# One ScalarE weight half moved ahead of two copies in both layers, another moved between the squares of the second mixer's norm

## The chip, the cores and the metric

The program runs on one core of a Trainium2 chip. The metric is device time in microseconds (us), smaller is better. Engines are called PE (TensorE matmul), DVE (VectorE), ACT (ScalarE), POOL (GpSimd) and SP (SyncE, which here only issues transfers). A wait in the queue of one engine holds everything that stands behind it in that queue, and nothing else.

## The reference, cut to what matters

Two blocks run one after the other on 256 tokens of width 1024. The first has two layers with three attention branches each, the second has two mixers; behind the first mixer stands a dense feed-forward net, behind the second a mixture of eight experts.

```python
for i in range(2):                                   # first block
    h = x @ w_in                                     # q, k, v and gates of three branches
    ya = moba_attention(...); yb = mla_attention(...); yc = diff_attention(...)
    merged = ga * (ya @ w_a) + gb * (yb @ w_b) + gc * (yc @ w_c)
    r = ALPHA * x + merged @ w_o
    x = layernorm(r + sigmoid(r @ w_pg) * (p_i @ w_p))
for i in range(2):                                   # second block
    h = rmsnorm(x, norm_mix[i])                      # squares, mean over 1024, x ** -0.5
    x = x + hybrid_mixer(h, w_in[i], ...)
    h = rmsnorm(x, norm_ffn[i])
    x = x + (swiglu(h, ...) if i == 0 else moe_swiglu(h, ...))
return rmsnorm(x, norm_final)
```

All of it is float32. The kernel multiplies float32 by splitting each operand into a high part (rounded by a copy to another format) and a low part (what the rounding left), and adding three products: high by high, high by low and low by high.

## The kernel before, in words

Everything is held feature by token: a tile has 128 features by 256 tokens, and x is eight such tiles. Weights come in units of 1 MB (1024 rows by 256 columns) through `ring`, which has three slots. SP issues one load per unit, in the order of use, each when the unit that is three places ahead in the ring has been read for good (`slot_freed`, which for a split unit is a count of its finished low parts). For each unit of 256 columns ACT makes the high part in two halves of 128 columns (`split`, one copy of 128x1024 each, signal `hi_done`). POOL makes the low parts of the layers and of the dense net (`low`, line 3092, signal `lo_done`), DVE those of the mixers. High and low parts have two places, so ACT may write the unit that is two ahead of the one that PE uses: `after("mc0")` is the copy of the unit two behind group `mc0`, which is `az0`. Its first half waits until PE has used the first half of `mc0`, its second until all of `mc0` is done, and both wait for the unit's load (`landed`).

The order on every engine is written out by hand. PE's order in a layer is the table `ORDER1`; the piece in question reads `("mc0"), ("B", 1), ("M", 0), ("V", 1), ("A", 2), ("mc1"), ("mc2"), ("B", 2)`. Here `B n` turns the probabilities of batch n (six or twelve transposes into PSUM), `M` is the second half of `mc0`, `V n` multiplies the turned probabilities `pT` with the values (into PSUM bank 7), and `A n` makes the scores. `scores(n)` writes bank 7 again with its last four matmuls, and so waits before them for `y_ready`: ACT's copy of the result of `V n-1` out of bank 7 (`take_y`). `pv(n)` waits for `pT_ready`: ACT's three copies of the turned probabilities (`take_turned`).

The second mixer's norm starts when the last dense unit is added up. DVE adds the sums to `xT` in four steps, ACT squares them (`square(j)`, 128x512), PE forms the mean with a matrix of 1/1024 in 16 records (`ms`), eight matmuls of zeros follow (`keep_busy(7, 8)`), ACT makes Ln and Exp (`inv_std`), DVE scales x to `h` tile by tile, ACT makes the high part of `h` in four pairs (`high_parts`), and PE's first group `gg` waits for each pair before it uses it (`split_project_first`). The half in question is the second half of the weights of `gv`, the group behind `gg`. The first half has been made at the end of the dense net's loop.

Of the kernel before, what the change touches and what calls it, by code (L numbers as in the profile page):

```python
# [62 lines left out]
LOG_EXP = "natural_log_exp_and_others"  # L63
# [196 lines left out]
def build_kernel(nc, a, out):  # L260

    ctx = ExitStack()
    with ctx:
# [9 lines left out]
        def signal(name, per=0):  # L273
            return Signal(sem(name), per)
# [220 lines left out]
        def views(b, n=2):  # L495
            return bank[b][:, :].rearrange("p (t s) -> p t s", t=n)
# [3 lines left out]
        FD = FF // S  # L500
# [23 lines left out]
        SPLITS_M = len(SPLIT2) + 3 * FD  # L524
# [53 lines left out]
        def _(sp):  # L578
# [107 lines left out]
        ff_full, ff_t, ff_g, ff_raw, ff_high, ff_h, ff_down = (signal(n) for n in (  # L686
            "ffn_full", "ffn_tanh", "ffn_gate_done", "ffn_hidden", "ffn_hidden_high", "ffn_h_ready", "ffn_down_done"))
# [980 lines left out]
        def _(act):  # L1668
# [3 lines left out]
            def copy(dst, src, scale=1.0):  # L1672
                return nc.scalar.activation(dst, src, ACT.Copy, scale=scale)  # L1673

            def split(slot, landed_at, q_slot, free, halves=(0, 1), width=P):


                act.wait_ge(landed[slot].h, landed_at)
                for t in halves:
                    if free:  # L1680
                        free(t)
                    copy(half_of(whi[:, q_slot, :], t, width), half_of(ring[:, slot, :], t, width)).then_inc(
                        hi_done.h, 1)
# [3 lines left out]
            def split1(layer, q, halves=(0, 1)):  # L1687

                n = split_unit(layer, q)

                def free(t):
                    if q >= 2:
                        turn, before = layer, SPLIT1[q - 2]
                    elif layer:
                        turn, before = layer - 1, SPLIT1[q - 2]
                    else:
                        return
                    if half_width(before) == S:
                        other = half_width((SPLIT1 + SPLIT1)[q]) != S
                        G1.wait_full(act, turn, before[:2] + str(int(before[2]) + (1 if other else t)))  # L1700
                    elif half_width((SPLIT1 + SPLIT1)[q]) == S:
                        G1.wait_full(act, turn, before)
                    elif t == 0 and before[1] != "v":
                        act.wait_ge(used.h, layer * len(SPLIT1) + q - 1)
                    else:
                        G1.wait_full(act, turn, before)
                split(n % RING, 16 * (n // RING + 1), q % 2, free, halves, half_width((SPLIT1 + SPLIT1)[q]))

            def drain(layer, name, dst, scale=1.0, rows=slice(0, P)):
                b = G1.wait_full(act, layer, name)  # L1710
                copy(dst, views(b)[rows], scale).then_inc(dr_a.h, 1)
# [4 lines left out]
            def inv_std(dst, src, e, log, at_log):  # L1716

                fn(dst, src, ACT.Ln, bias=eps[:, e:e + 1]).then_inc(log, 1)
                act.wait_ge(log, at_log)
                return fn(dst, dst, ACT.Exp, scale=-0.5)  # L1720
# [15 lines left out]
            def layer_body(layer):  # L1736
# [9 lines left out]
                def take_turned(n):  # L1746
                    act.wait_ge(p_turned.h, p_turned.at(layer, n + 1))
                    maps = 2 if BATCHES[n][0] == "diff" else 4
                    for i, b in enumerate((4, 5, 6)):
                        ins = copy(pT[:, 0:maps, i * P:(i + 1) * P],  # L1750
                                   bank[b][:, 0:maps * P].rearrange("p (m q) -> p m q", m=maps))
                    ins.then_inc(pT_ready.h, 1)

                def take_y(n):
                    kind, b = BATCHES[n]
                    act.wait_ge(pv_full.h, pv_full.at(layer, n + 1))
                    t0 = {"moba": 0, "mla": 4, "diff": 8}[kind] + 2 * b
                    copy(y[:, t0:t0 + 2, :], views(7)).then_inc(y_ready.h, 1)

                def after(name, halves=(0, 1)):  # L1760

                    split1(layer, SPLIT1.index(name) + 2, halves)
# [58 lines left out]
                drain(layer, "dv0", dv[:, :, 0:S])  # L1821
                after("dv1")
                drain(layer, "dv1", dv[:, :, S:512])
                take_turned(1)

                def latent(i):
                    b = G1.wait_full(act, layer, f"mc{i}")
                    copy(cq[:, 2 * i:2 * i + 2, :], views(b))
                    fn(gates[:, 2 * i:2 * i + 2, :], views(b), ACT.Square).then_inc(dr_a.h, 1)

                after("mc0")
                take_y(1)
                latent(0)
                exps(2)
                latent(1)
# [124 lines left out]
            def square(j):  # L1960

                return fn(sq[:, 2 * j:2 * j + 2, :], xT[:, 2 * j:2 * j + 2, :], ACT.Square)

            for layer in range(LAYERS):
                layer_body(layer)

            def split2(i, free, times=0, halves=(0, 1)):

                n = first_units + split_at2[i]
                split(n % RING, times + 16 * (n // RING + 1), i % 2, free, halves)  # L1970
# [38 lines left out]
            def high_parts(k):  # L2009

                for n in range(4):
                    act.wait_ge(h_part.h, h_part.at(k, n + 1))
                    copy(hh[:, 2 * n:2 * n + 2, :], h[:, 2 * n:2 * n + 2, :]).then_inc(hh_ready.h, 1)

            def mixer(m):
                def drained2_at(name):

                    return d2a.at(m, G2.nth(G2.index(name)))

                if m:  # L2020
                    for j in range(4):
                        act.wait_ge(x_up.h, j + 1)
                        square(j).then_inc(sq_ready.h, 1)
                    act.preload_act_table_set(LOG_EXP)
                b = G2.wait_full(act, m, "ms")
                inv_std(rs2[:, 0, :], views(b)[:, 0, :], 0, d2a.h, drained2_at("ms")).then_inc(std_ready.h, 1)
                if m:
                    split2(SPLITS_M + 1, lambda t: act.wait_ge(ff_down.h, 4 * FD), halves=(1,))
                high_parts(2 * m)
                high2(m, "xb0")  # L2030
                b = G2.wait_full(act, m, "gg")
# [84 lines left out]
            def norm(n):  # L2116
# [12 lines left out]
                if n == 1:  # L2129
                    high_ffn(0, (1,))  # L2130

            mixer(0)
            norm(1)
            high_parts(1)
# [36 lines left out]
            with act.Fori(0, FF_LOOP) as jj:  # L2171
# [6 lines left out]
                for k in range(3, 5):  # L2178
                    high_loop(jj, k)
                high_loop(jj, 5, (0,))  # L2180
            mixer(1)

            def token_squares(half, t, to):
# [1006 lines left out]
```

## Time and profile before

| what | us |
|---|---|
| median of three runs | 2121.65 |
| lowest and highest of the three | 2121.0 to 2123.34 |
| the profiled execution: its own time | 2121.3 |
| the profiled execution: span from first to last instruction | 2119.5 |
| PE busy in that span | 2096.3 (99%) |
| DVE, ACT, POOL busy | 1416.4, 1295.4, 651.4 |

The profile is one execution with the start, length and releaser of every instruction. Times in its rows are microseconds from the start of the span. A row of the order of time merges like instructions: start, length, engine, source line, operation, output<-input, count, and in brackets the idle time ahead of it with what ended it. Since line 720 is a helper that issues nearly every matmul, and line 1673 one that issues every ACT copy, rows are told apart by the names of what they write and read.

### The profile page before, as it was taken

How to read it: one execution, taken by the hardware profiler on the slowest of the kernel's cores; microseconds unless marked ns; L12 is line 12 of the kernel's file. 1: busy time of each engine (PE TensorE's matmuls, PEld its weight loads, DVE VectorE, ACT ScalarE, POOL GpSimd, SP SyncE). 2: the span in 40 equal slices, each digit the busy share in tenths (PEclk: the TensorE clock that was granted, in tenths of full speed). 3: DMA queues.
4: the chain of work that ended last, by engine and by line, in shares of the span. 5: the costliest groups of instructions: out<-in, count | busy, mean ns of one | idle time of the engine just before them, and what ended most of it. 6: DMA issues, size and time to landing. Idle time of an engine off the chain costs nothing.

```text
span 2119.5 us, 33547 instructions
## 1 busy us (share of the span) xinstructions
PE 2096.3 (99%) x13311; PEld 1867.1 (88%) x13315; DVE 1416.4 (67%) x1437; ACT 1295.4 (61%) x1424; POOL 651.4 (31%) x316
## 2 busy tenths in 40 slices
PE   9999999999999999999999999999999999999998
PEld 8979999988999999999998888888888888888887
DVE  1555223346422774223777999999999999999997
ACT  4556545455544534444545777777777777777776
POOL 5717886726787204988101000000000000000000
PEclk9999999999999999999999999999999999999999
DMA  7434564625455425655447999999999999999995
GB/s 245 138 105 153 179 198 156 183 75 163 160 188 177 129 91 175 189 193 178 141 140 252 387 376 336 370 360 376 352 351 370 351 375 351 359 356 375 367 365 200
DMA packets 307633, 529.06 MB, mean 250 GB/s; under 512 B 11842, under 2 KB 152802, under 8 KB 307520
## 3 DMA queue, kind: packets, MB, share of 16 engines
q1 hardware_dynamic: 306496, 525.92, 70.9%
q8 instruction: 84, 1.38, 0.3%
q0 software_dynamic: 736, 1.00, 0.2%
q10 hardware_dynamic: 288, 0.52, 0.1%
q14 instruction: 29, 0.24, 0.0%
HBM read 525.84 MB, written 1.05 MB: 249 GB/s over the span
## 4 chain that ended last, share of the span: by engine, by line
PE 90%; POOL 3%; DVE 3%; ACT 2%; DMA 1%; issue 1%; SPq 0%; DVEq 0%; POOLq 0%
PE bank L720 88%; POOL weights_low L3092 3%; PE bank L1525 1%; DVE qb L2354 1%; DMA ring<-in_w_in_dram 1%; ACT sc L1670 1%; ACT weights_high L1673 0%; DVE sc L2362 0%; DMA ring<-in_w_ple_dram 0%; DVE h L2362 0%; PE bank L929 0%; PE bank L731 0%; DVE nmax L2389 0%; ACT expert_weights_high L1673 0%; ACT xT L1670 0%
## 5 line engine op out<-in xcount | busy, mean ns | idle before, releaser
L2354 DVE TENSOR_TENSOR expert_weights_low<-ring_experts,expert_weights_high 128x2048 fp32r<-128x2048 f32 x336 | 764.7, 2288 | 72.6 <-ACT expert_weights_high L1673 72.5
L1673 ACT ACTIVATE expert_weights_high<-ring_experts 128x2048 fp32r<-128x2048 f32 x336 | 646.4, 1924 | 166.3 <-PE bank L720 162.2
L3092 POOL TENSOR_TENSOR weights_low<-ring,weights_high 128x1024 fp32r<-128x1024 f32 x252 | 617.5, 2474 | 332.0 <-ACT weights_high L1673 218.8
L1673 ACT ACTIVATE weights_high<-ring 128x1024 fp32r<-128x1024 f32 x294 | 303.9, 1056 | 331.7 <-PE bank L720 293.0
L720 PE MATMUL bank<-x_high,weights_high 128*128 128x256 f32 x1024 | 229.8, 281 | 0.5 <-POOL weights_low L3092 0.4
L720 PE MATMUL bank<-x_high,weights_low 128*128 128x256 f32 x1024 | 226.2, 277 | 0.0
L720 PEld LDWEIGHTS bank<-x_high,weights_high 128*128 128x128 f32 x1024 | 183.6, 188 | 2.5 <-POOL weights_low L3092 0.8
L720 PEld LDWEIGHTS bank<-x_high,weights_low 128*128 128x128 f32 x1024 | 183.3, 188 | 0.5 <-issue 0.5
L720 PE MATMUL bank<-expert_weights_high,gathered_high 128*128 128x512 f32 x456 | 180.7, 396 | 0.4 <-DVE gathered_low L2362 0.4
L720 PE MATMUL bank<-expert_weights_high,gathered_low 128*128 128x512 f32 x456 | 177.8, 390 | 0.0
L720 PE MATMUL bank<-expert_weights_high,gathered_high_b 128*128 128x512 f32 x448 | 177.6, 396 | 0.0
L720 PE MATMUL bank<-expert_weights_high,gathered_low_b 128*128 128x512 f32 x448 | 174.7, 390 | 0.0
L720 PE MATMUL bank<-expert_weights_high,hidden_turned_low 128*128 128x512 f32 x440 | 171.3, 389 | 0.0
L720 PE MATMUL bank<-expert_weights_high,hidden_turned_high 128*128 128x512 f32 x440 | 171.2, 389 | 0.0
L720 PE MATMUL bank<-h_high,weights_high 128*128 128x256 f32 x704 | 164.0, 283 | 5.1 <-ACT h_high L1673 5.1
L720 PE MATMUL bank<-h_high,weights_low 128*128 128x256 f32 x704 | 161.6, 281 | 0.0
L720 PEld LDWEIGHTS bank<-h_high,weights_high 128*128 128x128 f32 x704 | 131.1, 192 | 7.7 <-ACT weights_high L1673 2.9
L720 PE MATMUL bank<-x_low,weights_high 128*128 128x256 f32 x1024 | 137.4, 277 | 0.0
L720 PEld LDWEIGHTS bank<-h_high,weights_low 128*128 128x128 f32 x704 | 130.6, 192 | 0.0
L720 PEld LDWEIGHTS bank<-x_low,weights_high 128*128 128x128 f32 x1024 | 126.3, 188 | 0.0
L720 PE MATMUL bank<-expert_weights_low,gathered_high 128*128 128x512 f32 x456 | 122.3, 390 | 0.0
L720 PE MATMUL bank<-expert_weights_low,gathered_high_b 128*128 128x512 f32 x448 | 120.0, 390 | 0.0
(338 smaller groups left out, 3724.7 us busy)
## 6 DMA issues: line engine op xcount, KB each, us to landing
ring_experts<-in_moe_w_gate_dram SPq DMA_DIRECT2D x112, 1024.0 KB, 6.0
ring_experts<-in_moe_w_up_dram SPq DMA_DIRECT2D x112, 1024.0 KB, 5.8
ring_experts<-in_moe_w_down_dram SPq DMA_DIRECT2D x112, 1024.0 KB, 5.4
ring<-in_w_in_dram SPq DMA_DIRECT2D x62, 1024.0 KB, 5.3
ring<-in_w_merge_dram SPq DMA_DIRECT2D x24, 1024.0 KB, 5.1
ring<-in_w_out_dram SPq DMA_DIRECT2D x14, 1024.0 KB, 5.1
ring<-in_ffn_w_gate_dram SPq DMA_DIRECT2D x11, 1024.0 KB, 5.4
ring<-in_ffn_w_up_dram SPq DMA_DIRECT2D x11, 1024.0 KB, 5.3
```

What stands on the lines that cost most here:

```text
L720: ins = pe.matmul(dst, w, x, start=start, stop=stop, skip_group_check=share)
L1525: ins = pe.transpose(bank[2][:, c * P:(c + 1) * P], hd[:, c * P:(c + 1) * P], ident)
L1670: return nc.scalar.activation(dst, src, func, **kw)
L1673: return nc.scalar.activation(dst, src, ACT.Copy, scale=scale)
L2354: return nc.vector.tensor_tensor(dst, x, z, op)
L3092: nc.gpsimd.tensor_tensor(half_of(wlo[:, q_slot, :], t, width), half_of(ring[:, slot, :], t, width), half_of(whi[:, q_slot, :], t, width). ...
```

## The change

Two places on ACT change. In both layers the first half of the copy for `az0` moves ahead of the three copies of turned probabilities, and the copy of y moves ahead of the second half. In the second mixer the load of the table for Ln and Exp moves ahead of the squares, and the second half of the weights of `gv` moves from behind the Exp to between the second and the third square.

```diff
                 drain(layer, "dv1", dv[:, :, S:512])
+                after("mc0", (0,))
                 take_turned(1)
+                take_y(1)
+                after("mc0", (1,))
 ...
-                after("mc0")
-                take_y(1)
                 latent(0)
                 exps(2)
...
                 if m:
+                    act.preload_act_table_set(LOG_EXP)
                     for j in range(4):
                         act.wait_ge(x_up.h, j + 1)
                         square(j).then_inc(sq_ready.h, 1)
-                    act.preload_act_table_set(LOG_EXP)
+                        if j == 1:
+                            split2(SPLITS_M + 1, lambda t: act.wait_ge(ff_down.h, 4 * FD), halves=(1,))
                 b = G2.wait_full(act, m, "ms")
                 inv_std(rs2[:, 0, :], views(b)[:, 0, :], 0, d2a.h, drained2_at("ms")).then_inc(std_ready.h, 1)
-                if m:
-                    split2(SPLITS_M + 1, lambda t: act.wait_ge(ff_down.h, 4 * FD), halves=(1,))
                 high_parts(2 * m)
```

On ACT, in a layer, from the copy of `dv1` on, the order before is this. `w_landed2` is the load of the unit of `az0`, `probs_turned` is `B 1` on PE, and `pv_full` is `V 1` on PE.

```order
L1673 ACTIVATE dv<-bank0 128x512 [waits group_full]
L1673 ACTIVATE pT<-bank4 128x4x128 [waits probs_turned]
L1673 ACTIVATE pT<-bank5 128x4x128
L1673 ACTIVATE pT<-bank6 128x4x128
L1673 ACTIVATE weights_high<-ring 128x8x128 [waits split_half_used,w_landed2]
L1673 ACTIVATE weights_high<-ring 128x8x128 [waits group_full]
L1673 ACTIVATE y<-bank7 128x512 [waits pv_full]
L1673 ACTIVATE cq<-bank1 128x512 [waits group_full]
```

With the change the same stretch of ACT reads:

```order
L1673 ACTIVATE dv<-bank0 128x512 [waits group_full]
L1673 ACTIVATE weights_high<-ring 128x8x128 [waits split_half_used,w_landed2]
L1673 ACTIVATE pT<-bank4 128x4x128 [waits probs_turned]
L1673 ACTIVATE pT<-bank5 128x4x128
L1673 ACTIVATE pT<-bank6 128x4x128
L1673 ACTIVATE y<-bank7 128x512 [waits pv_full]
L1673 ACTIVATE weights_high<-ring 128x8x128 [waits group_full,w_landed2]
L1673 ACTIVATE cq<-bank1 128x512 [waits group_full]
```

The copy that waits for the load of `az0` now stands ahead of the copies to `pT`, and only its second half stands behind the copy to `y`.

On ACT at the start of the second mixer the order before is this. `x_updated` is DVE's sum, `ffn_down_done` the last matmuls of the dense net on PE.

```order
L1670 ACTIVATE sq<-xT 128x512 [waits x_updated] x4
L2024 ACT_TABLE_LOAD
L1670 ACTIVATE rs<-bank,eps 128x256 [waits group2_full]
L1670 ACTIVATE rs<-rs 128x256 [waits drained2_by_scalar]
L1673 ACTIVATE weights_high<-ring 128x8x128 [waits ffn_down_done,w_landed1]
L1673 ACTIVATE h_high<-h 128x512 [waits h_tiles_ready] x4
```

With the change the same stretch reads:

```order
L2022 ACT_TABLE_LOAD
L1670 ACTIVATE sq<-xT 128x512 [waits x_updated] x2
L1673 ACTIVATE weights_high<-ring 128x8x128 [waits ffn_down_done,w_landed1]
L1670 ACTIVATE sq<-xT 128x512 [waits x_updated] x2
L1670 ACTIVATE rs<-bank,eps 128x256 [waits group2_full]
L1670 ACTIVATE rs<-rs 128x256 [waits drained2_by_scalar]
L1673 ACTIVATE h_high<-h 128x512 [waits h_tiles_ready] x4
```

The table load and the weight half both stand ahead of the mean now. No instruction is added or removed on any engine, and the other engines keep their order.

## Rows read from the trace of the kernel before

**Rows 1.** The page: the chain that ended last, its shares by engine.

```profile
PE 90%; POOL 3%; DVE 3%; ACT 2%; DMA 1%; issue 1%; SPq 0%; DVEq 0%; POOLq 0%
```

**Rows 2.** The chain in order of time, layer 0: start, length, what.

```profile
88.17 5.57 POOL weights_low L3092 x2
...
93.75 5.21 DMA ring<-in_w_in_dram
```

**Rows 3.** ACT in order of time, layer 0.

```profile
94.99 1.58 ACT L1673 ACTIVATE pT<-bank 128x512 f32<-128x512 f32 x3 [1.50 <-PE bank L929]
98.99 2.00 ACT L1673 ACTIVATE weights_high<-ring 128x1024 fp32r<-128x1024 f32 x2 [2.43 <-DMA ring<-in_w_in_dram]
100.90 0.58 ACT L1673 ACTIVATE y<-bank 128x512 f32<-128x512 f32 x1
...
106.36 0.51 ACT L1670 ACTIVATE sc<-sc,nmax 128x256 f32<-128x256 f32 x1 [3.90 <-DVE nmax L2390]
```

**Rows 4.** PE in order of time, layer 0.

```profile
97.62 1.57 PE L720 MATMUL bank<-pT,av 128*64 128x256 f32 x16
99.12 1.57 PE L720 MATMUL bank<-dqk 64*128 64x256 f32 x12
101.53 0.71 PE L720 MATMUL bank<-dqk 64*128 64x128 f32 x4 [0.84 <-ACT y L1673]
```

**Rows 5.** The same stretch of layer 1: one row of ACT.

```profile
436.74 2.00 ACT L1673 ACTIVATE weights_high<-ring 128x1024 fp32r<-128x1024 f32 x2 [2.51 <-DMA ring<-in_w_in_dram]
```

**Rows 6.** The same stretch of layer 1: two rows of PE.

```profile
435.28 1.57 PE L720 MATMUL bank<-pT,av 128*64 128x256 f32 x16
...
439.28 0.71 PE L720 MATMUL bank<-dqk 64*128 64x128 f32 x4 [0.93 <-ACT y L1673]
```

**Rows 7.** ACT in order of time, start of the second mixer.

```profile
995.31 1.06 ACT L1673 ACTIVATE weights_high<-ring 128x1024 fp32r<-128x1024 f32 x1 [1.66 <-PE bank L720]
996.71 2.67 ACT L1670 ACTIVATE sq<-xT 128x512 f32<-128x512 f32 x4 [0.34 <-DVE xT L2354]
999.40 1.28 ACT L2024 ACT_TABLE_LOAD   x1
...
1002.31 1.04 ACT L1673 ACTIVATE weights_high<-ring 128x1024 fp32r<-128x1024 f32 x1
```

**Rows 8.** PE in order of time, start of the second mixer.

```profile
997.83 3.61 PE L720 MATMUL bank<-sq,ones 128*128 128x256 f32 x16
...
1004.21 0.71 PE L720 MATMUL bank<-h_high,weights_high 128*128 128x256 f32 x4 [1.03 <-ACT h_high L1673]
1007.00 0.84 PE L720 MATMUL bank<-h_high,weights_high 128*128 128x256 f32 x4 [2.09 <-ACT h_high L1673]
...
1013.74 0.28 PE L720 MATMUL bank<-h_high,weights_high 128*128 128x256 f32 x1
```

**Rows 9.** DVE and POOL in order of time there, and DVE's `h` by tile.

```profile
995.99 2.73 DVE L2354 TENSOR_TENSOR xT<-xT,bank 128x512 f32<-128x512 f32 x4 [4.75 <-PE bank L720]
1002.52 5.35 DVE L2362 SCALAR_TENSOR_TENSOR h<-xT,q,rs 128x256 f32<-128x256 f32 x8 [3.41 <-ACT rs L1670]
...
1003.43 2.57 POOL L3092 TENSOR_TENSOR weights_low<-ring,weights_high 128x1024 fp32r<-128x1024 f32 x1 [4.58 <-ACT weights_high L1673]
...
L2362 DVE SCALAR_TENSOR_TENSOR h<-xT,q,rs x8: 471/474/2572, 1002.5 to 1007.4; 128x256 f32<-128x256 f32 x8
```

**Rows 10.** PE in order of time, the same norm in the first mixer.

```profile
695.93 0.74 PE L720 MATMUL bank<-h_high,weights_high 128*128 128x256 f32 x4
...
701.26 0.28 PE L720 MATMUL bank<-h_high,weights_high 128*128 128x256 f32 x1
```

**Rows 11.** Stretches: length, busy (count) of PE, PEld, DVE, ACT, POOL; PE's granted clock, DMA share, GB/s.

```profile
681.00:684.00 3.00, 1.47 (x8) 1.27 (x8) 2.48 (x4) 2.61 (x5) 3.00 (x3) 1.00 0.77 268
1004.00:1007.00 3.00, 0.71 (x4) 0.53 (x4) 3.00 (x3) 0.69 (x2) 2.00 (x1) 1.00 0.00 0
1009.00:1010.00 1.00, 1.00 (x7) 1.00 (x7) 1.00 (x3) 0.00 (x0) 0.00 (x0) 0.50 0.06 16
```

## The prediction

> **What bounds the kernel now.** I first read the chain that ended last: 90% of it is PE, the rest small pieces of other engines [rows 1]. So time is won or lost only where PE waits. Both edited places touch such waits. In layer 0 the chain leaves PE for a piece of 13 us (88.17 to 101.53): POOL makes the low parts of `mc0`, which frees the ring slot, and the load of `az0` starts at 93.75 and takes 5.21, so it is there at 98.96 [rows 2]. The reader is to see in ACT's own order that the copies to `pT` were made long before that, at 94.99, and that ACT then waited 2.43 for the load, copied two weight halves, and only then y at 100.90 [rows 3]. PE used `pT` at 97.62, made the first twelve matmuls of the next scores from 99.12, and stood 0.84 until y was out of bank 7 [rows 4]. Layer 1 shows the same, with 0.93 [rows 5, 6]. In the second mixer ACT's last copy of the dense net ends at 996.37, the squares run from 996.71, then the table load, and the weight half follows behind the Exp at 1002.31 [rows 7]. PE waits 1.03 for the first pair of `h_high` and 2.09 for the second [rows 8]. DVE shows why: one of the eight `h` instructions took 2572 ns where the median is 474, and it lies beside POOL's `weights_low` of 1003.43 to 1006.00, which is the low part of that weight half [rows 9].
>
> **The change, the layers.** The first weight half now stands ahead of the copies to `pT`, and it needs the load, which nothing here makes earlier (PE's use, POOL's low parts and the load itself all come from work ahead of the edit). So ACT stands at it until 98.99. Behind it in ACT's queue are the copies to `pT`, for which PE waits, and y.
> - One half takes 2.00 / 2 = 0.96 as a step (y follows the two at 100.90). So the copies to `pT` run from 99.95 to 99.95 + 1.58 = 101.53, and with 0.04 of signal PE starts `V 1` at 101.57 in place of 97.62: 3.95 late.
> - `V 1` ends 1.57 later at 103.14. ACT copies y at once, some 0.5, until 103.65. PE's last four score matmuls come 3.07 after the start of `V 1` (97.62 to 101.53 less the wait of 0.84), at 104.64, so y is there and the old wait of 0.84 is gone. Against 101.53 the loss is 3.1.
> - Layer 1: 436.74 + 0.96 + 1.58 + 0.04 = 439.32 against 435.28, then + 3.07 = 442.39 against 439.28: again 3.1 [rows 5, 6].
> - The second weight half now follows y, at some 103.7 to 104.7; its low part (POOL) ends near 107.1 and is first used in `az0`, behind all of `mc1` and `mc2`. ACT's next work for the critical chain, the exponentials, started at 106.36 and will start near 109.5 [rows 3], so the copies of `mc0` and its squares, some 1 us, are still hidden. If that cover were gone, the price would be the 0.96 of the half.
> - Nothing takes the 3.1 back: PE is busy from there to `B 2`, and what follows is released by it.
>
> **PE's clock in the layers.** This is the cost that the trace doesn't show at this place. PE will now stand for some 3.9 us between the end of `M` and `V 1`. In the mixer, 3 us with 0.71 of PE work at the full clock (2.4 GHz) were followed by a stretch at half of it (1.2 GHz); 3 us with 1.47 of work were not [rows 11]. The new pause holds no work at all, and so is nearer to the first. The price of one such stretch: the piece from the second pair to the next group took 1013.74 - 1007.00 = 6.74 with it [rows 8] and 701.26 - 695.93 = 5.33 without, in the same norm of the first mixer [rows 10], so 1.41. From below the price is zero (the clock stays), from above it is 1.41, or twice that if the slow stretch lasts longer. Since part of it may fall into the pause itself, I take 1.1 for each layer, 2.2 in all. The Trainium skill (TensorE: Matmul & The Clock Gate, Part 1: The HAM clock gate) says that the array's clock is halved after recent idleness and that where this falls against the program differs from run to run. By that rule each new pause would lower the clock; the trace agrees at 1004 to 1010, and no row here has a pause as long as the new ones.
>
> **The change, the second mixer.**
> - The table load, hidden until now behind the mean, comes ahead of the squares. ACT is free at 996.37, the load takes 1.28, so the squares start at 997.66 and not 996.71. Each takes 2.67 / 4 = 0.67: the first is done at 998.33, the second at 999.0.
> - The weight half follows, to 999.95; its wait for the dense net's last matmul is met (PE left it at 997.83). The third square is done at 1000.62, the fourth at 1001.29.
> - PE's mean takes 3.61 / 4 = 0.90 a pair [rows 8]: from 998.37, the second pair at 999.27, the third waits from 1000.17 to 1000.66, the fourth at 1001.56, the end at 1002.46. Before it ended at 1001.44: 1.02 late. Ln, Exp, DVE's `h` and the first pair on PE go 1.02 later, to 1003.54 for `h` and 1005.23 for PE.
> - POOL's low part starts with the end of the half, near 1000.1, and with 2.57 ends near 1002.7, ahead of `h`. DVE is then not held. In the first mixer, where it was not, the second pair followed 0.70 behind the first, so PE takes it at 1005.93 and not at 1007.00: 1.07 won.
> - PE's pause is now one of 1 us, so the slow stretch should not come: another 1.41 won. In all 2.5.
>
> DVE's additions to `xT` ran beside a POOL low part before (995.99 to 998.72) and took 2.73 for four, 0.68 each: instructions with one input in PSUM are not held by POOL [rows 9]. The scores of the layers also have one input in PSUM, so the later POOL half there holds nobody. The Trainium skill (SBUF, Who interferes with whom) says the same: a VectorE instruction with two SBUF inputs blocks against a GpSimd instruction that reads SBUF, for the whole of it, and one with a single SBUF input does not. By its rule the gain in the mixer is the whole hold, as in the sum.
>
> **Sum.** 2 x 3.1 + 2.2 - 2.5 = +5.9. The profiled execution took 2121.3 (span 2119.5), 0.35 below the median of the three runs, so the changed kernel should show a span near 2125.4, a time of 2127.2 for that execution and a median near 2127.5. A measurement of this kernel tells 0.2% (4.2 us) from no change.
>
> **The rivals.**
> - *The clock holds in the layers.* PE's pause there costs only itself: 6.2 - 2.5 = +3.7, 2125.4, within 0.2%. For it: a pause with somewhat more work in it, 1.47 in 3 us, cost nothing, so the two are not far apart, and where the pause falls may differ. Against: the pause that did cost a stretch had more work in it than the new ones. 15%.
> - *Nothing is won in the mixer.* POOL's low part still lies beside `h`, or the slow stretch comes there anyway because of the later squares: 6.2 + 2.2 - 0 = +8.4, 2130. It decides where POOL starts later than 1001. Against: the half's load landed long ago (its first half was copied at 995.31), and nothing else stands in POOL's queue there. 10%.
> - *Faster: the load is no hindrance.* If the load of `az0` landed by the time `B 1` is done (94.99), the copies to `pT` would be 0.96 later, which PE, busy until 97.62, would hardly feel, y would be out early, and 0.84 + 0.93 + 2.5 = 4.3 would be won: 2117.4. In a layer the change breaks even if the load lands by 98.96 - 3.1 = 95.9. Against: it starts at 93.75 and took 5.21. 5%.
> - *The forecast itself*, both kinds of cost and the gain: 70%. Its own range is 2125.5 to 2129.2, from clock prices of 0.3 to 2 a layer.
>
> **How the numbers follow.** Slower by over 0.2% holds the forecast but for its lowest edge and the second rival: 0.79. Within 0.2%: the first rival and that edge, 0.16. Faster: 0.05. The range reaches down to the first rival's upper part and up to the second: 2124.3 to 2130.2.
>
> **What the changed profile would show.** In both layers ACT's `pT` copies at 99.95 and near 442 (437.70 plus the 4.2 that layer 0 loses), behind one weight half; PE idle for 3.9 ahead of `V 1`, released by ACT's `pT`; no wait for y; a granted clock of 0.5 for a few us behind it. In the mixer a table load ahead of the squares, two short waits of PE for squares, no `h` instruction above 500 ns, no wait of 2 us for `h_high`, full clock in `gg`. It would be wrong if the load landed earlier, if PE's wait were filled by something that I take for fixed, or if the table load or the half delayed the mean by more than 1 us.

## The result, and the profile after

| | before | with the change |
|---|---|---|
| median, us | 2121.17 | 2126.46 |
| lowest to highest of 18 runs | 2118.45 to 2124.62 | 2122.16 to 2129.78 |
| span of the profiled execution | 2119.5 | 2124.0 |

The ratio is 1.0026, with a 95% interval of 1.0020 to 1.0032: the change costs 5.3 us (2126.46 - 2121.17), and clearly so. Forecast were 5.9, and a median near 2127.5 in a range of 2124.3 to 2130.2; the median is 2126.46. The two profiled executions differ by 4.5.

Of the profile after, ACT in order of time in layer 0 answers to [rows 3] (start, length, engine, line, operation, and the idle time ahead with its end):

```profile
99.89 1.06 ACT L1673 ACTIVATE weights_high<-ring 128x1024 fp32r<-128x1024 f32 x1 [5.73 <-DMA ring<-in_w_in_dram]
100.85 1.55 ACT L1673 ACTIVATE pT<-bank 128x512 f32<-128x512 f32 x3
105.29 0.60 ACT L1673 ACTIVATE y<-bank 128x512 f32<-128x512 f32 x1 [2.89 <-PE bank L720]
105.79 1.05 ACT L1673 ACTIVATE weights_high<-ring 128x1024 fp32r<-128x1024 f32 x1
...
111.37 0.51 ACT L1670 ACTIVATE sc<-sc,nmax 128x256 f32<-128x256 f32 x1 [3.56 <-DVE nmax L2391]
```

PE in the same stretch, to be held against [rows 4]; the last row is the first matmul of the next group, `mc1`:

```profile
97.28 1.07 PE L720 MATMUL bank<-x_high,weights_low 128*128 128x256 f32 x8
102.46 2.80 PE L720 MATMUL bank<-pT,av 128*64 128x256 f32 x16 [4.10 <-ACT pT L1673]
105.19 2.06 PE L720 MATMUL bank<-dqk 64*128 64x256 f32 x16
107.18 0.39 PE L720 MATMUL bank<-x_high,weights_high 128*128 128x256 f32 x1
```

And PE in layer 1, against [rows 6]:

```profile
443.97 2.88 PE L720 MATMUL bank<-pT,av 128*64 128x256 f32 x16 [3.96 <-ACT pT L1673]
446.78 1.93 PE L720 MATMUL bank<-dqk 64*128 64x256 f32 x16
448.65 0.39 PE L720 MATMUL bank<-x_high,weights_high 128*128 128x256 f32 x1
```

ACT now stands at the load for 5.73, and the copies to `pT` that were made at 94.99 come at 100.85. PE waits 4.10 and 3.96 for them, and does not wait for y any more. Stretches of the profile after (length, busy of PE, PEld, DVE, ACT, POOL, then PE's granted clock, DMA share, GB/s; PEld is PE's loading of weights) show the price behind the pause:

```profile
98.00:102.00 4.00, 0.35 (x4) 0.15 (x2) 0.00 (x0) 2.11 (x4) 2.05 (x2) 1.00 0.53 168
...
103.00:106.00 3.00, 3.00 (x20) 2.14 (x18) 0.00 (x0) 0.71 (x2) 0.36 (x1) 0.50 0.00 0
...
444.00:447.00 3.00, 3.00 (x18) 2.03 (x20) 0.00 (x0) 0.11 (x1) 0.88 (x1) 0.50 0.00 0
```

In both layers PE works at 1.2 GHz (granted clock 0.50) right behind the pause. The profile before had 2.4 GHz (1.00) in the same places:

```profile
97.00:102.00 5.00, 4.16 (x39) 3.40 (x37) 0.00 (x0) 3.01 (x5) 3.28 (x2) 1.00 0.50 155
...
437.45:440.87 3.42, 2.49 (x22) 2.13 (x19) 0.85 (x3) 2.75 (x5) 3.00 (x2) 1.00 0.25 78
```

The start of the second mixer, ACT in order of time, against [rows 7]:

```profile
1004.64 1.28 ACT L2022 ACT_TABLE_LOAD   x1
1005.94 1.15 ACT L1670 ACTIVATE sq<-xT 128x512 f32<-128x512 f32 x2
1007.00 1.04 ACT L1673 ACTIVATE weights_high<-ring 128x1024 fp32r<-128x1024 f32 x1
1007.94 1.14 ACT L1670 ACTIVATE sq<-xT 128x512 f32<-128x512 f32 x2
```

PE there, against [rows 8]:

```profile
1006.62 3.98 PE L720 MATMUL bank<-sq,ones 128*128 128x256 f32 x16 [0.38 <-ACT sq L1670]
1010.66 1.67 PE L827 MATMUL bank<-zeros 128*128 128x512 bf16 x7
1013.36 1.44 PE L720 MATMUL bank<-h_high,weights_high 128*128 128x256 f32 x8 [1.03 <-ACT h_high L1673]
```

DVE and POOL there, against [rows 9]:

```profile
1011.68 3.25 DVE L2363 SCALAR_TENSOR_TENSOR h<-xT,q,rs 128x256 f32<-128x256 f32 x8 [4.31 <-ACT rs L1670]
...
1008.12 2.35 POOL L3093 TENSOR_TENSOR weights_low<-ring,weights_high 128x1024 fp32r<-128x1024 f32 x1 [1.03 <-ACT weights_high L1673]
```

POOL's low part ends at 1010.47, before DVE starts on `h`, whose eight instructions now take 3.25 and not 5.35. The first and the second pair of `gg` are one row of eight matmuls, with no wait between them.

### The profile page after: what moved, and what is told of

Read it like the earlier page. It is cut to its first block, busy times and chain, and to the rows that moved or that the text cites. A ratio compares the mean times of both kernels' runs of the same rounds, so it can differ in the third digit from the quotient of the medians.

```text
span 2124.0 us, 33549 instructions
## 1 busy us (share of the span) xinstructions
PE 2094.9 (99%) x13311; PEld 1863.8 (88%) x13315; DVE 1414.0 (67%) x1437; ACT 1294.5 (61%) x1424; POOL 653.3 (31%) x316
## 4 chain that ended last, share of the span: by engine, by line
PE 90%; POOL 3%; DVE 3%; ACT 2%; DMA 1%; issue 1%; SPq 0%; DVEq 0%; POOLq 0%; ACTq 0%
PE bank L720 88%; POOL weights_low L3093 3%; PE bank L1525 1%; DVE qb L2355 1%; DMA ring<-in_w_in_dram 1%; ACT sc L1670 1%; DMA ring<-in_w_ple_dram 0%; DVE sc L2363 0%; ACT weights_high L1673 0%; PE bank L929 0%; PE bank L731 0%; DVE nmax L2390 0%; ACT expert_weights_high L1673 0%; ACT xT L1670 0%; DVE h L2363 0%
```

## The experiments

All were timed beside the kernel before, in three groups (e1 to e4; e5 to e7; e8 and e9). Each ratio is to the kernel before of its own group, and 0.001 of it is 2.1 us.

| run | what | ratio | 95% interval |
|---|---|---|---|
| e1 | layers alone | 1.0034 | 1.0022 to 1.0046 |
| e2 | second mixer alone | 0.9989 | 0.9980 to 0.9998 |
| e3 | the change, pause filled | 1.0012 | 1.0003 to 1.0021 |
| e4 | `pT`, y, then both halves | 0.9983 | 0.9974 to 0.9992 |
| e5 | table load alone | 1.0002 | 0.9993 to 1.0011 |
| e6 | mixer's pause filled | 0.9995 | 0.9986 to 1.0004 |
| e7 | e4 and e9 together | 0.9966 | 0.9954 to 0.9978 |
| e8 | `pT`, half, y, half | 0.9994 | 0.9985 to 1.0003 |
| e9 | mixer's half alone | 0.9992 | 0.9983 to 1.0001 |

**e1, the layers alone.** The part of the diff in the layers, on the kernel before.

```diff
+                after("mc0", (0,))
                 take_turned(1)
+                take_y(1)
+                after("mc0", (1,))
...
-                after("mc0")
-                take_y(1)
```

> The edit in the layers alone; the second mixer is as before. My theory (each layer loses 3.1 by the late copies to pT and some 1.1 by a slow stretch of PE behind the new pause): 2 x 4.2 = 8.4 us slower than before, ratio 1.0040. The rival without a price of the clock: 6.2 us, 1.0029. Two pauses of PE of about 4 us released by ACT's pT, none of 2 us fewer at h_high than before (2.09 stays).

Median 2128.49 against 2120.86, by the ratio 7.2 us slower, with an interval that holds both 6.2 and 8.4: the timing alone doesn't separate the two theories (with a price of the clock, and without). The trace does. PE in the profile of e1, layer 0 and the mixer:

```profile
102.76 2.46 PE L720 MATMUL bank<-pT,av 128*64 128x256 f32 x16 [4.09 <-ACT pT L1673]
...
107.49 0.38 PE L720 MATMUL bank<-x_high,weights_high 128*128 128x256 f32 x1
...
1012.56 0.71 PE L720 MATMUL bank<-h_high,weights_high 128*128 128x256 f32 x4 [1.03 <-ACT h_high L1673]
1015.35 1.22 PE L720 MATMUL bank<-h_high,weights_high 128*128 128x256 f32 x4 [2.09 <-ACT h_high L1673]
```

From `V 1` to `mc1` it takes 4.73, as after the change (4.72), where a run without a slow stretch takes 3.12 (e3 and e4 below), and the mixer's two waits are untouched. Stretches of the same profile show that the slow clock behind the mixer's pause lasted twice as long here as in the profile before:

```profile
1015.00:1018.00 3.00, 2.65 (x12) 2.65 (x13) 3.00 (x8) 1.56 (x3) 0.00 (x0) 0.50 0.19 11
1018.00:1021.00 3.00, 3.00 (x16) 3.00 (x15) 0.63 (x2) 0.00 (x0) 2.18 (x4) 0.50 0.02 5
```

**e2, the second mixer alone.** The part of the diff in the mixer, on the kernel before.

```diff
                 if m:
+                    act.preload_act_table_set(LOG_EXP)
...
-                    act.preload_act_table_set(LOG_EXP)
+                        if j == 1:
+                            split2(SPLITS_M + 1, lambda t: act.wait_ge(ff_down.h, 4 * FD), halves=(1,))
...
-                if m:
-                    split2(SPLITS_M + 1, lambda t: act.wait_ge(ff_down.h, 4 * FD), halves=(1,))
```

> The edit in the second mixer alone; the layers are as before. My theory: 2.5 us faster (1.1 of it the hold of DVE that is gone, 1.4 the slow stretch that does not come), ratio 0.9988. The rival that nothing is won there (the later squares eat it): ratio 1.0. The rows: no h instruction over 500 ns, PE's waits for h_high near 1 us in place of 1.03 and 2.09.

Median 2118.17, by the ratio 2.3 us faster (interval 0.4 to 4.2), near the 2.5 expected, and the rival falls, though narrowly by time. DVE's `h` by tile in this profile (minimum/median/maximum in ns):

```profile
L2362 DVE SCALAR_TENSOR_TENSOR h<-xT,q,rs x24: 476/480/486, 693.0 to 1004.1; 128x256 f32<-128x256 f32 x24
```

The one instruction of 2572 ns [rows 9] is gone. So the change consists of a part that wins 2.3 and a part that loses 7.2; their sum, 4.9, is near the 5.3 of the whole.

**e3, the change with its new pause filled.** In `pv`:

```diff
                     kind, b = BATCHES[n]
+                    if n == 1:
+                        keep_busy(7, 14)
```

> The whole change, and in both layers fourteen matmuls of zeros into bank 7 (free there) between M and V 1, some 3.4 us that lie in the new pause of 3.9. If the pause costs a slow stretch of the clock, the stretch is gone and the kernel is 2.2 us faster than the change as it is, that is 3.7 us slower than before, 1.0017. If the clock there costs nothing (the loss is the wait alone), it stays at the 5.3 us of the change, 1.0025. The start of V 1 must not move.

Ratio 1.0012: filling the pause with useless work makes the changed kernel 3.0 us faster (1.0026 - 1.0012, of 2121), where 2.2 were expected. The two ratios come from different groups and their intervals just touch, so the size of the 3.0 is rough; the trace gives it closer. PE in layer 0 of this profile:

```profile
98.46 2.97 PE L827 MATMUL bank<-zeros 128*128 128x512 bf16 x13
102.26 1.57 PE L720 MATMUL bank<-pT,av 128*64 128x256 f32 x16 [0.83 <-ACT pT L1675]
103.77 1.68 PE L720 MATMUL bank<-dqk 64*128 64x256 f32 x16
105.38 0.38 PE L720 MATMUL bank<-x_high,weights_high 128*128 128x256 f32 x1
```

`V 1` still waits for `pT` and comes about as late as without the filling, but from there to `mc1` it is 3.12 in place of 4.72; in layer 1 it is 3.11 in place of 4.68, and neither layer has a slow stretch. The price of the slow stretch is thus 1.6 a layer, and it is the emptiness of the pause that brings it.

**e4, y ahead of both weight halves, `pT` left where it was.**

```diff
                 take_turned(1)
+                take_y(1)
+                after("mc0")
...
-                after("mc0")
-                take_y(1)
```

> Layers alone, the other way round: the copies to pT stay first, then y, then both weight halves of az0; the mixer is as before. If the harm of the change is only that pT stands behind the load, y can go ahead at no cost: PE's waits of 0.84 and 0.93 for y go, 1.8 us faster than before, ratio 0.9992. The rival: az0's parts come late by 0.7 us and PE or the loads behind them lose it again, ratio 1.0.

Ratio 0.9983, 3.6 us faster, twice what was expected; 1.8 lies just inside the interval (1.7 to 5.5). PE and ACT in layer 0:

```profile
98.38 1.57 PE L720 MATMUL bank<-pT,av 128*64 128x256 f32 x16
99.88 1.68 PE L720 MATMUL bank<-dqk 64*128 64x256 f32 x16
101.50 0.39 PE L720 MATMUL bank<-x_high,weights_high 128*128 128x256 f32 x1
...
99.99 0.60 ACT L1673 ACTIVATE y<-bank 128x512 f32<-128x512 f32 x1 [2.66 <-PE bank L720]
100.49 2.00 ACT L1673 ACTIVATE weights_high<-ring 128x1024 fp32r<-128x1024 f32 x2
```

From `V 1` to `mc1` it is 3.12, where the kernel before took 4.55 (97.62 to 102.17, its `mc1`): a wait of 0.84 had cost 1.43. The bracket counts from the end of the twelve matmuls that PE had already made, and leaves out that in a run without the stop the last four follow before that end. In layer 1 it is 3.11 against 4.64. That is 2.96 in all. The halves of `az0` come at 100.49, later than before, and nothing of it is lost.

**e5, the table load alone.** Second mixer, the weight half back behind the Exp.

```diff
                 if m:
+                    act.preload_act_table_set(LOG_EXP)
                     for j in range(4):
                         act.wait_ge(x_up.h, j + 1)
                         square(j).then_inc(sq_ready.h, 1)
-                    act.preload_act_table_set(LOG_EXP)
```

> Second mixer alone: the table load moves ahead of the squares, the weight half stays behind the Exp. My theory: the load, hidden until now, makes the squares 0.9 late and the mean 0.4 to 0.6 late, while DVE is still held by POOL and PE's waits of 1.0 and 2.1 for h_high stay: 0.5 us slower than before, ratio 1.0002. The rival (the early table load is what wins, since Ln starts sooner): 0 to 1 us faster.

Ratio 1.0002, no difference that can be told: the interval holds the 0.5 expected and also a gain of up to 1.5, so the time alone leaves the rival open. The trace speaks against it: the mean starts late, and from the dense net's last matmul to `gg` it is 7.13 (996.94 to 1004.07) against 6.49 before (997.72 to 1004.21). Both waits are there. PE:

```profile
997.59 3.72 PE L720 MATMUL bank<-sq,ones 128*128 128x256 f32 x16 [0.38 <-ACT sq L1670]
...
1004.07 0.71 PE L720 MATMUL bank<-h_high,weights_high 128*128 128x256 f32 x4 [1.03 <-ACT h_high L1673]
1006.87 0.74 PE L720 MATMUL bank<-h_high,weights_high 128*128 128x256 f32 x4 [2.09 <-ACT h_high L1673]
```

And stretches around that pause:

```profile
1004.00:1007.00 3.00, 0.84 (x5) 0.66 (x6) 3.00 (x4) 0.65 (x2) 1.87 (x1) 1.00 0.01 1
1007.00:1012.00 5.00, 5.00 (x42) 4.89 (x43) 3.15 (x6) 1.25 (x2) 1.67 (x3) 1.00 0.12 9
```

Here the same pause as in the kernel before was followed by no slow stretch at all. The layers' experiments e4 and e8 have this pause too; a stretch behind it in e4, then one in e8:

```profile
1004.00:1009.00 5.00, 5.00 (x25) 5.00 (x25) 2.62 (x5) 0.71 (x2) 2.19 (x4) 0.50 0.03 4
...
1006.00:1009.00 3.00, 3.00 (x17) 3.00 (x16) 2.08 (x4) 0.33 (x1) 0.74 (x2) 0.50 0.03 5
```

So behind this pause the clock fell for 3.4 us in two profiles (before, e8), for 6.8 in two (e1, e4), and not at all in one (e5).

**e6, the mixer's pause filled in the kernel before.** `fill` is the number of the mixer, passed for `gg` alone.

```diff
+                        if fill and kk == 2:
+                            keep_busy(7, 8)
                         if kk % 2 == 0:
                             wait_high(kk // 2)
```

> The kernel before, and in the second mixer eight matmuls of zeros into bank 7 (free there) on PE between the first and the second pair of gg, 1.9 us in the wait of 2.1. DVE is held by POOL as before, so the second pair of gg must come at the same time (2.8 behind the first); what goes is the slow stretch behind it, if the pause is what brings it. My theory: 1.4 us faster (one slow stretch of 3.4 us) to 3 (where it lasts 6.8, as in two of the profiles since), ratio 0.9990. The rival, that the slow stretch has another cause or costs nothing: ratio 1.0, half clock still behind 1007.

Ratio 0.9995 with an interval that holds 1: inconclusive by time. The trace shows the expected picture. PE:

```profile
1000.96 0.71 PE L720 MATMUL bank<-h_high,weights_high 128*128 128x256 f32 x4 [1.03 <-ACT h_high L1675]
1001.51 1.90 PE L829 MATMUL bank<-zeros 128*128 128x512 bf16 x8
1003.76 0.74 PE L720 MATMUL bank<-h_high,weights_high 128*128 128x256 f32 x4 [0.35 <-ACT h_high L1675]
```

The second pair comes 2.80 behind the first, as before (the hold of DVE is untouched), the next group comes 5.33 behind it in place of 6.74, and no slow stretch follows. Since it does not follow every time in the kernel before either (e5), this one profile does not prove that the filling keeps it away.

**e8, `pT`, one half, y, the other half.** Layers alone: the change without the step that puts the half ahead of `pT`.

```diff
                 take_turned(1)
+                after("mc0", (0,))
+                take_y(1)
+                after("mc0", (1,))
...
-                after("mc0")
-                take_y(1)
```

> Layers alone, the edit without its first line's harm: the copies to pT stay first, then the first weight half (which waits for the load), then y, then the second half. If only the place of pT behind the load harms, the rest of the edit wins: y is out near 100.5 and the first part of the scores ends at 100.7, so PE's stop for y is gone or below 0.1, and with it some 1.4 us a layer: 2.8 faster than before, ratio 0.9987, like e4. The rival, that y must stand ahead of both halves to win anything: ratio 1.0.

Ratio 0.9994, 1.3 us faster, with an interval (0.6 slower to 3.2 faster) that holds both the 2.8 expected and nothing: the time does not decide between them. The trace does. PE in layer 0:

```profile
98.07 1.57 PE L720 MATMUL bank<-pT,av 128*64 128x256 f32 x16
99.57 2.34 PE L720 MATMUL bank<-dqk 64*128 64x256 f32 x16
101.84 0.39 PE L720 MATMUL bank<-x_high,weights_high 128*128 128x256 f32 x1
```

From `V 1` to `mc1` it is 3.77 against 3.12 in e4 and 4.55 before, and in layer 1 it is 3.60 (434.44 to 438.04) against 4.64: 1.8 won in all, so both theories were off: y gains without standing ahead of both halves, but less than 2.8. My estimate had taken the end of the drained row (100.7) for the time at which PE wants y. Before and in e8 `mc1` starts 0.69 behind the end of y's copy, and without a stop 3.12 behind `V 1`, so PE wants y 2.43 behind `V 1`, some 0.6 earlier than that. But the point of the run stands: with `pT` ahead of the load this edit doesn't lose, with `pT` behind it (e1) it loses 7.2.

**e9, the weight half alone in the second mixer.** The half between the squares, the table load behind them.

```diff
                         square(j).then_inc(sq_ready.h, 1)
+                        if j == 1:
+                            split2(SPLITS_M + 1, lambda t: act.wait_ge(ff_down.h, 4 * FD), halves=(1,))
                     act.preload_act_table_set(LOG_EXP)
...
-                if m:
-                    split2(SPLITS_M + 1, lambda t: act.wait_ge(ff_down.h, 4 * FD), halves=(1,))
```

> Second mixer alone: the weight half between the squares as in the change, the table load behind the squares as before. My theory: DVE's hold goes (2.1 of wait) and the mean comes at most 0.2 late, so 2.1 to 2.4 us are won by the wait and the mean of some 1 to 1.4 by slow stretches that come in part of the executions: 3.5 us faster than before, ratio 0.9984, about 0.9 better than the change's own mixer. The rival, that the table load has to stand first: no better than e2 (0.9989).

Ratio 0.9992, 1.7 us faster, and its interval holds both the 3.5 expected and the 2.3 of e2: whether the place of the table load matters is not told by time, nor whether the edit wins at all. In the trace PE's mean starts without a wait. PE:

```profile
996.84 3.88 PE L720 MATMUL bank<-sq,ones 128*128 128x256 f32 x16
...
1003.48 1.43 PE L720 MATMUL bank<-h_high,weights_high 128*128 128x256 f32 x8 [1.03 <-ACT h_high L1673]
```

From the dense net's last matmul to `gg` it is 6.76 here (996.72 to 1003.48), 7.39 after the change (1005.97 to 1013.36) and 6.49 before: with the table load behind the squares `gg` comes 0.63 sooner than with it in front, not 0.9, and is 0.27 late.

**e7, the better halves together.** The layers of e4 with the mixer of e9, no other line changed.

> A version that takes what the runs so far point to: in the layers pT, then y, then both halves; in the second mixer the weight half between the squares as in the change, but the table load behind the squares. Layers: 2 x 1.45 won (e4's trace: the wait for y and the restart of PE behind it). Mixer: the 2.6 of the change plus the 0.9 by which its mean came late. In all 2.9 + 3.5 = 6.4 us faster than before, ratio 0.9970. If the table load behind the squares delays Ln instead, 0.9 less.

Median 2113.96 against 2120.58, ratio 0.9966 (0.9954 to 0.9978): 7.2 us faster than before (interval 4.7 to 9.8, which holds the 6.4 expected) and some 12.7 faster than the change, the best version of this study. PE's waits for y are gone, and its largest wait for `h_high` is 1.03.

## Why the prediction was right, step by step

- **What bounds it, and where the loss comes from: shown.** e1 and e2 part the change into a loss in the layers and a gain in the mixer. e8 differs from e1 in nothing but the place of `pT`, ahead of the load or behind it, and so shows that the loss hangs on this move. All marks that the prediction named for the layers are in the profile after, at the foretold places.
- **`V 1` 3.95 late: 4.17 and 4.02.** In layer 0 PE starts `V 1` at 102.46 where 97.62 + 0.67 was due (this execution is 0.67 late from its start on, from its first loads). Of the 4.17, 0.23 are the load, which starts at 94.42 and is 5.44 long in this profile. The first copy to `pT` comes at 100.85, the foretold 99.95 with these two delays.
- **The old wait for y, 0.84 and 0.93: mis-sized, 1.43 and 1.53.** I took the idle time in the bracket as its whole price, and put the last four matmuls 3.07 behind `V 1`. e4 measured what a run without the stop needs, 3.12 to `mc1` in place of 4.55.
- **The clock, 1.1 a layer out of 0 to 1.41: mis-sized, 1.60 and 1.57** (4.72 and 4.68 against the 3.12 of e3 and e4). It lies above the upper bound for one stretch; the row that gave 1.41 is of other matmuls. The prediction took 1.1 because part of the slow stretch might fall into the pause. Next to none did: in the profile after it begins within 0.2 of `V 1` in both layers (at 102.6 and 443.9) and is 3.4 long. e3 took it away by filling the pause, so the cause is shown. The first rival (the clock holds) falls.
- **The second weight half is hidden: as foretold.** In layer 0 it ends at 106.84, and ACT still idles 3.56 before the exponentials at 111.37.
- **The layers in all, 8.4: 4.34 + 4.06 = 8.40 in the profile,** 7.2 by e1's timing. That this sum was exact is luck: two errors of 0.5 to 0.6 a layer, one of each sign, cancel.
- **The mixer, 2.5: 2.6 in the profile.** The squares went faster than 0.67 each, since they were no longer paced by DVE (1.15 for two), so the first pair comes 0.90 late and not 1.02; the hold's end gives 2.09 between the pairs, and from the second pair to the next group it is 5.33 in place of 6.74, as foretold. Of the two short waits of PE for squares only one shows, 0.38 ahead of the mean; the other can be no more than the 0.37 by which the mean grew (3.98 against 3.61). The second rival (nothing won) falls by e2.
- **What was not foreseen is how the mixer's 1.41 is spread.** The slow stretch there came in four of five profiles with that pause, and cost nearly nothing, 1.4 or 2.6 (from the second pair to the next group: 6.74 before and in e8, 8.00 in e1, 7.91 in e4). The gain of an execution, reckoned from these, thus lies between 1.2 and 3.8. The measured 5.3 is 8.4 less 3.1, inside that. That the filling of this pause (e6) or the shorter pause (e2, e9) keeps the slow stretch away fits every profile, but one profile of each does not prove it.
- **The two profiled executions differ by 4.5, not 5.3,** because they differ elsewhere too: +0.67 at the start, and -1.5 in the group `dt` of the second mixer, behind which the profile before has a slow stretch and the one after has none; the rest, some -0.4, is in smaller drifts. The first lies ahead of every edit. The slow stretch at `dt` came in six of the eleven profiles, with the change (e3) and without it, so it is not the change's doing; it is a reason why medians, and not two profiles, give the size.
- **The faster rival** (the load is there in time) falls: the load landed at 99.86, within 1 us of its time before (98.96).
- **A slip in the range:** clock prices of 0.3 to 2 a layer give 2125.9 to 2129.3, not the 2125.5 to 2129.2 that the prediction has for the forecast itself. The measured median lies in both.

## What to carry to other kernels

In a queue that is written by hand, an instruction that waits for a transfer belongs behind everything that is ready and that someone waits for: moving one copy of 1 us ahead of three ready ones made what waits for them 4 us late, because it took its wait along. Price a wait of PE by what the engine does from the work ahead of it to the work behind it, with and without the stop, and not by the idle time in the row; and where a pause like those here opens (4 us empty, or 1.03 and 2.09 with four matmuls between), add the slow stretch that can follow it. Before judging a bundle of moves, time them apart: here a gain of 2.3 lay hidden under a loss of 7.2, and another order of the same copies (e4) would have won 3.6.

## What the runs showed of the hardware

- Behind the same pause of PE (1.03 and 2.09 idle with four matmuls between) the granted clock fell to 1.2 GHz for 3.4 us, for 6.8 us, or not at all, in executions of code that is the same there. Behind the longer, empty pauses of 3.69 to 4.10 us it fell for 3.4 us in all four cases profiled (both layers, after and e1). The Trainium skill (TensorE: Matmul & The Clock Gate, Part 1: The HAM clock gate) says that it differs from run to run where the slow time falls against the program; the runs agree.
- A stop of PE costs more than its idle time: 0.84 of idle cost 1.43, and 0.93 cost 1.53, here between matmuls of 64 rows.
- The DVE instruction that met POOL's subtraction waited for all of the rest of it (2572 to 2581 ns, and not 474), in every profile in which the two met (before, e1, e4, e5, e6, e8), and in none in which POOL was done first (after, e2, e3, e7, e9: at most 486 ns). That is what the Trainium skill (SBUF — State Buffer, Who interferes with whom) says of a VectorE instruction with two SBUF inputs.
